# Two memory steps to a round from the ninth round on, memory scores kept to two PSUM banks, gate rows turned four to six steps earlier

## The chip, the cores and the metric

The kernel runs on one core of a Trainium2 chip. The metric is the device time of one launch in microseconds (us). The engines are called by their names and by the short names of the profile: TensorE (PE, its weight loads PEld), VectorE (DVE), ScalarE (ACT), GpSimd (POOL) and SyncE (SP), which issues most of the transfers.

## The reference, cut to what matters

The reference is a stack of three layers on 512 tokens of width 1024. The change touches the mixer of the last one only:

```
h = modulate(rms_norm(x, norm_mix_g), sh1, sc1)
q_a, k_a, v_a, qk_m, v_m, o_m, gates = split(h @ w_in)
y_attn = axial_gqa_attention(q_a, k_a, v_a, ...)      # 8 heads of 64, full softmax over 512 keys
y_mem = bidirectional_mlstm(qk_m, v_m, o_m, gates, ...)  # 4 heads of 128, forward and backward
mix = concatenate([y_attn, y_mem]) @ w_out
x = x + g1 * mix

# mLSTM of one head and direction, in its parallel form, as the kernel computes it:
F = cumsum(log_sigmoid(f)); M = cummax(i - F)
score[s, t] = (k[s] . q[t]) * 128**-0.5 * exp(i[s] - F[s] - M[t])   # where s is not past t
y[t] = (score[:, t] @ v) / max(|sum_s score[s, t]|, exp(-(F[t] + M[t])))
```

## The kernel before, in words

All engines run one program each, written in one order by hand; they meet only through semaphores, and each engine takes its own instructions in order. Tokens lie in T = 4 row blocks of 128.

**The projection w_in.** It is computed as a run of matrix products, in this order: k2 (8 blocks), conv 0 and 1 (4 blocks), og (8 blocks), conv 2 and 3 (4 blocks), v2 (8 blocks). A block is 12 matmuls of 512 columns in k2, og and v2 (lines 596 to 598; k2 is narrower) and 24 in conv (lines 622 to 624). After each block every engine takes one step of a generator `small_jobs` of 32 steps, numbered 0 to 31, so og holds steps 12 to 19, conv 2 and 3 steps 20 to 23, and v2 steps 24 to 31. In these steps sit: turning the gate rows on TensorE (`gates`, line 1104, steps 17 and 18) after VectorE wrote the log of the forget gates ("lf", line 2552, step 12); copying them on ScalarE (steps 18 and 19); the two scans of each direction on VectorE (`gates`, lines 2515 to 2525, steps 24 and 26), the SiLU of the convolutions on ScalarE (line 1681, steps 15 and 25), turning the gate columns on TensorE (`gate_columns`, lines 1114 and 1115, steps 28 and 30), their copy and exp on ScalarE (lines 1669 and 1670, steps 29 and 31), and the first two steps of attention (steps 28 and 30).

**Attention (`heads`).** A step u of `attend("B")` on TensorE issues two score products of 512 columns (line 848), the turning of two exponentiated score rows of step u-2 (line 857, `turn_p`) and, when u is odd, the product with v for two row blocks (line 873). VectorE takes the row maximum bound of the two scores (line 2148) and copies one of the turned rows (line 2163), ScalarE does exp (line 1436) and the other copy (line 1380). There are 16 pairs of scores, and TensorE has 21 steps in all. VectorE's write of a score row waits for the turning of the row four before it, in the same step of TensorE.

**Memory (`memory`).** Eight passes m (head and direction, even m forward, odd m backward) of four steps t. Step (m, t) on TensorE issues the score product of row block t (`score`, line 1168; 512, 384, 256, 128 columns for t = 0 to 3 when m is even, the other way round when m is odd), at t = 0 and 2 the outcome of the pass before for two row blocks (`outcome`, line 1182), and at t = 2 the broadcast of the next running maximum (`start`, line 1160). On VectorE, step (m, t) is `weigh` (lines 2607 and 2610: score times decay, read from the bank), at t = 1 and 3 also `divide` of the pass before (lines 2619, 2621, 2629 or 2632: it reads the outcome's bank), and at t = 3, ahead of `weigh`, `own` of the next pass (line 2592). ScalarE makes the decays (lines 1763 and 1770), GpSimd masks the diagonal (line 2863).

**The round.** `side_by_side` takes one step of `heads` and one of `memory` in turn on each engine until both have ended. Rounds are numbered here from 0, so round n has attention step u = n + 2 and, on all engines, memory step k = n - 1, where k = 4m + t. Attention ends on TensorE with round 18, and 18 memory steps follow alone.

**PSUM banks.** A bank is taken as the least recently used of a set: attention's scores and turned rows from banks 0 to 3, its outcome from 4, the running maximum from 5, and memory's scores and outcomes from 6 and 7. Once `heads` has ended on TensorE (`busy` is empty), memory's scores and outcomes are taken from banks 0 to 4, 6 and 7 (`B_LATE`). Before writing into a bank, TensorE waits for the engine that read its last user: `weigh` for a score, the second half of `divide` for an outcome.

**Weight chunks.** A weight chunk of 128x2048 is split by ScalarE (line 1278) and VectorE (line 1906) into two halves. In `memory` at step k = 12 both engines prepare one chunk ahead for the product that follows (`cur.reach(high, 2)`, `cur.reach(low, 2)`).

Of the kernel before, what the change touches and what calls it, by code (L numbers as in the profile page):

```python
# [188 lines left out]

def side_by_side(heads, mem, over):  # L190

    live = [heads, mem]
    while live:
        for job in (heads, mem):
            if job in live and next(job, over) is over:
                live.remove(job)


def weight_plan(a_w_in, a_w_o, b_w_in, b_w_o, mlp_w_up, mlp_w_down, w_ada_2, w_in_2, w_out_2, w_gate_2, w_up_2, w_down_2):
# [98 lines left out]
def program(nc, x, positions, a_w_in, a_w_o, b_w_in, b_w_a2, b_b_a, b_g_norm, b_w_o, ln_mix_g, ln_mix_b,  # L298
# [4 lines left out]
    with ctx:  # L303
# [169 lines left out]

        LAG = 2

        B_UNITS, B_OUT, B_MAX, B_MEM, B_LATE, ANY = range(4), (4,), (5,), (6, 7), (0, 1, 2, 3, 4, 6, 7), range(8)

        DIVIDED = {"A": 7, "B": 4}

# [70 lines left out]
        def tensor_program(pe):  # L550
# [572 lines left out]
            def small_jobs():  # L1123
                for step in range(32):
                    if step == 10:
                        turn("qT2", tm, 4, s_step.at("rope q"))
                    if step in (17, 18):
                        gates(step - 17)
                    if step == 20:
                        turn("kT2", kd2, 2, s_step.at("rope k"))  # L1130
                    if step in (28, 30):
                        gate_columns((step - 28) // 2)
                    if step in (28, 30):
                        next(heads)
                    yield
# [8 lines left out]
            gemm_tok("v2", 512, "x4", 1, among=range(4, 8))  # L1144
            drain(jobs)

            busy = ["heads"]

            def until_done(heads):
                yield from heads  # L1150
                busy.clear()

            def memory():
                def start(m):
                    hh, d = MEM[m]
                    b = banks.take(("M", m), False, B_MAX)
                    sel = ident[32 * d:32 * d + 4, 32 * d + hh:32 * d + hh + 1].broadcast_to([4, P])
                    w.wait_ge(*banks.free(("M", m), s_act.sem))
                    w.wait_ge(*s_step.at(("Mr", d)))
                    pe.matmul(bank[b][:, :], sel, Mr[d], start=True, stop=True).then_inc(*s_mm.up(("M", m)))  # L1160

                def score(m, t):
                    hh = MEM[m][0]
                    c0, c1_ = keys(m, t)
                    b = banks.take(("S", m, t), False, B_MEM if busy else B_LATE)
                    w.wait_ge(*banks.free(("S", m, t), s_act.sem))
                    w.wait_ge(*s_act.at(("conv", 7)))
                    pe.matmul(bank[b][:, 0:c1_ - c0], mqk[:, 4 + hh, t * P:(t + 1) * P], mqk[:, hh, c0:c1_],
                              start=True, stop=True).then_inc(*s_mm.up(("S", m, t)))

                def outcome(m, tt):
                    hh, d = MEM[m]
                    b = banks.take(("hm", m, tt), False, B_MEM if busy else B_LATE)
                    w.wait_ge(*banks.free(("hm", m, tt), s_act.sem))
                    w.wait_ge(*s_step.at(("ST", m, T - 1)))
                    w.wait_ge(*s_act.at(("v2", T - 1)))
                    w.wait_ge(*s_step.at("vx1"))
                    for t in (2 * tt, 2 * tt + 1):
                        src = list(range(0, t + 1) if d == 0 else range(t, T))
                        o = (t % 2) * 256  # L1180
                        for q in src:
                            step = pe.matmul(bank[b][:, o:o + 130], STm[m % 2][:, q, t * P:(t + 1) * P], vx[:, q, hh, :],
                                             start=q == src[0], stop=q == src[-1])
                    step.then_inc(*s_mm.up(("hm", m, tt)))

# [11 lines left out]
            side_by_side(until_done(heads), memory(), jobs)  # L1197
# [54 lines left out]
        def scalar_program(act):  # L1252
# [430 lines left out]
            def small_jobs():  # L1683
                for step in range(32):
# [15 lines left out]
                    if step in (18, 19):  # L1700
                        gates(step - 18)
# [4 lines left out]
                    if step in (29, 31):  # L1706
                        gate_columns((step - 29) // 2)
                    if step in (28, 30):
                        next(heads)
                    yield  # L1710
# [158 lines left out]
        def vector_program(dve):  # L1869
# [667 lines left out]
            def small_jobs():  # L2537
                for step in range(32):
# [18 lines left out]
                    if step in (24, 26):  # L2557
                        gates((step - 24) // 2)
                    if step in (28, 30):
                        next(heads)  # L2560
                    yield
# [437 lines left out]
```

## Time and profile before

| | us |
|---|---|
| median of 3 runs | 1908.58 |
| lowest and highest | 1908.34 and 1909.94 |
| the profiled execution, its own time | 1908.34 |
| its span in the profile | 1906.6 |
| PE busy | 1848.9 (97%) |
| DVE busy | 1151.6 (60%) |
| ACT busy | 734.6 (39%) |
| POOL busy | 108.8 (6%) |

The profiled execution took 1908.34 us, 1.74 us more than its span, and 0.24 us less than the median. The chain that ended last runs for 77% of the span over TensorE, for 15% over VectorE and for 4% over ScalarE. TensorE's granted clock was 0.994 over the span. The attention and memory rounds lie between 1363.6 and 1476.2 us of the span; the products of w_in before them.

### The profile page before, as it was taken

Reading aid. Unit: us, or ns where it says so; the run is one execution under the profiler, and the core shown is the slowest. Engines: PE = TensorE matmul, PEld = TensorE weight load, DVE = VectorE, ACT = ScalarE, POOL = GpSimd, SP = SyncE. Lnnn points to the kernel's source line nnn. Section 1 sums busy time; section 2 is a strip of 40 time slices with the busy share of each in tenths; the row PEclk is TensorE's granted clock in tenths of the full one; section 3 lists DMA queues with packets and bytes.
Section 4 is the critical chain, followed back from the end, with each engine's and each line's share of the span. In section 5 each row is a group of like instructions: output and inputs, shape, how many; then the busy total and the mean of one; then the engine's idle time right before and its main releaser. Section 6 shows DMA issues by size and latency. Waiting matters only on the chain.

```text
span 1906.6 us, 22855 instructions
## 1 busy us (share of the span) xinstructions
PE 1848.9 (97%) x9156; PEld 1495.3 (78%) x9156; DVE 1151.6 (60%) x2038; ACT 734.6 (39%) x1155; POOL 108.8 (6%) x109
## 2 busy tenths in 40 slices
PE   9999999999999999999999999899988999999997
PEld 7775888878888888878888888688655798888885
DVE  4987676555557686567554544976666554333438
ACT  4458352233233434544322222365554352222221
POOL 0341000000000152000000000000001000000000
PEclk9999999999999999999999999999999999999999
DMA  6221425433432121233434343122100313223221
GB/s 207 67 72 35 161 89 173 158 133 133 149 138 91 62 72 45 66 133 107 137 112 131 111 132 111 46 90 88 67 17 28 100 34 121 89 95 104 89 89 45
DMA packets 119018, 187.24 MB, mean 98 GB/s; under 512 B 7664, under 2 KB 72400, under 8 KB 115840
## 3 DMA queue, kind: packets, MB, share of 16 engines
q1 hardware_dynamic: 117520, 180.96, 28.9%
q0 software_dynamic: 1392, 4.82, 0.8%
q8 instruction: 72, 1.18, 0.3%
q14 instruction: 34, 0.28, 0.0%
HBM read 183.62 MB, written 2.15 MB: 97 GB/s over the span
## 4 chain that ended last, share of the span: by engine, by line
PE 77%; DVE 15%; ACT 4%; issue 3%; DMA 1%; POOL 0%; DVEq 0%; SPq 0%; ACTq 0%; POOLq 0%
PE bank L622 10%; PE bank L624 10%; PE bank L623 10%; PE bank L815 7%; PE bank L813 7%; PE bank L814 7%; PE bank L596 2%; PE bank L598 2%; PE bank L597 2%; DVE wl L1906 2%; PE bank L873 2%; DVE gb L2259 2%; PE bank L848 2%; PE bank L857 2%; DVE m L2257 1%
## 5 line engine op out<-in xcount | busy, mean ns | idle before, releaser
L1906 DVE TENSOR_TENSOR wl<-raw,wh 128x2048 fp32r<-128x2048 f32 (+1 forms) x137 | 308.2, 2254 | 190.7 <-ACT wh L1278 190.1
L1278 ACT ACTIVATE wh<-raw 128x2048 fp32r<-128x2048 f32 (+1 forms) x142 | 265.1, 1882 | 227.9 <-PE bank L815 90.4
L622 PE MATMUL bank<-xh,wh 128*128 128x512 f32 (+1 forms) x872 | 343.0, 393 | 4.0 <-DVE wl L1906 4.0
L623 PE MATMUL bank<-xh,wl 128*128 128x512 f32 (+1 forms) x872 | 342.2, 392 | 0.0
L624 PE MATMUL bank<-xl,wh 128*128 128x512 f32 (+1 forms) x872 | 342.2, 392 | 0.0
L815 PE MATMUL bank<-wh,ul 128*128 128x512 f32 x592 | 230.5, 389 | 0.0
L814 PE MATMUL bank<-wl,uh 128*128 128x512 f32 x592 | 230.4, 389 | 0.0
L813 PE MATMUL bank<-wh,uh 128*128 128x512 f32 x592 | 230.4, 389 | 0.0
L622 PEld LDWEIGHTS bank<-xh,wh 128*128 128x128 f32 (+1 forms) x872 | 163.5, 187 | 43.2 <-DVE wl L1906 5.1
L624 PEld LDWEIGHTS bank<-xl,wh 128*128 128x128 f32 (+1 forms) x872 | 163.5, 187 | 37.4
L623 PEld LDWEIGHTS bank<-xh,wl 128*128 128x128 f32 (+1 forms) x872 | 163.5, 187 | 36.7
L596 PE MATMUL bank<-wh,xh 128*128 128x512 f32 (+1 forms) x352 | 138.3, 393 | 1.7 <-DVE wl L1906 1.7
L2073 DVE TENSOR_TENSOR h<-h,bank 128x512 f32<-128x512 f32 x112 | 75.4, 683 | 105.1 <-PE bank L815 102.1
L1400 ACT ACTIVATE A<-bank 128x512 f32<-128x512 f32 x64 | 38.2, 596 | 259.0 <-PE bank L624 255.4
L598 PE MATMUL bank<-wh,xl 128*128 128x512 f32 (+1 forms) x352 | 134.1, 381 | 0.0
L597 PE MATMUL bank<-wl,xh 128*128 128x512 f32 (+1 forms) x352 | 133.9, 380 | 0.0
L814 PEld LDWEIGHTS bank<-wl,uh 128*128 128x128 f32 x592 | 111.1, 188 | 23.3
L813 PEld LDWEIGHTS bank<-wh,uh 128*128 128x128 f32 x592 | 111.2, 188 | 23.2
L815 PEld LDWEIGHTS bank<-wh,ul 128*128 128x128 f32 x592 | 111.1, 188 | 23.2
L2082 DVE TENSOR_TENSOR A<-A 128x512 f32<-128x512 f32 x64 | 44.1, 689 | 93.7 <-ACT A L1400 93.4
L1380 ACT ACTIVATE A<-bank 128x512 f32<-128x512 f32 (+4 forms) x106 | 51.4, 489 | 88.8 <-PE bank L598 32.3
L596 PEld LDWEIGHTS bank<-wh,xh 128*128 128x128 f32 x352 | 66.2, 188 | 16.6 <-issue 2.6
(352 smaller groups left out, 2962.6 us busy)
## 6 DMA issues: line engine op xcount, KB each, us to landing
raw<-in_mlp_w_up SPq DMA_DIRECT2D x32, 1024.0 KB, 5.6
raw<-in_mlp_w_down SPq DMA_DIRECT2D x32, 1024.0 KB, 5.1
raw<-in_w_ada SPq DMA_DIRECT2D x24, 1024.0 KB, 5.0
raw<-in_b_w_in SPq DMA_DIRECT2D x12, 1024.0 KB, 5.3
raw<-in_w_gate SPq DMA_DIRECT2D x11, 1024.0 KB, 5.3
raw<-in_w_up SPq DMA_DIRECT2D x11, 1024.0 KB, 5.5
raw<-in_w_in SPq DMA_DIRECT2D x10, 1024.0 KB, 5.1
raw<-in_w_down SPq DMA_DIRECT2D x10, 1024.0 KB, 5.0
```

The costliest lines, as they stand in the source:

```text
L596: pe.matmul(o, X, H[:, k, :], start=kk == 0, stop=False)
L597: pe.matmul(o, X, L[:, k, :], start=False, stop=False)
L598: step = pe.matmul(o, Y, H[:, k, :], start=False, stop=kk == 7)
L622: pe.matmul(o, H[:, k, c], xh[:, k, :], start=k == 0, stop=False)
L623: pe.matmul(o, L[:, k, c], xh[:, k, :], start=False, stop=False)
L624: step = pe.matmul(o, H[:, k, c], xl[:, k, :], start=False, stop=k == 7)
L813: pe.matmul(o, X, H[:, f, :], start=f == 0, stop=False)
L814: pe.matmul(o, X, L[:, f, :], start=False, stop=False)
L815: step = pe.matmul(o, Y, H[:, f, :], start=False, stop=f == nf - 1)
L1278: act.activation(slots[slot_of[i]][0][:, 0:n], raw[:, i % NRAW, 0:n], ACT.Copy).then_inc(*s_high.up(i))
L1906: dve.tensor_tensor(L[:, 0:n], raw[:, i % NRAW, 0:n], H[:, 0:n].bitcast(F), ALU.subtract).then_inc(*s_low.up(i))
L2073: dve.tensor_tensor(hv, hv, ps, ALU.add).then_inc(*s_row.up(name))
```

## The change

Three edits, on all engines that have a part in them:

1. `side_by_side` takes one memory step to an attention step in the first eight rounds and two from round 8 on.
2. The set `B_LATE` is gone: memory's scores and outcomes are taken from banks 6 and 7 to the end, also when attention has ended.
3. In `small_jobs`, TensorE turns the gate rows in steps 13 and 14 (17 and 18 before) and the gate columns in steps 22 and 26 (28 and 30); ScalarE copies the rows in steps 14 and 15 (18 and 19) and does the columns in steps 23 and 27 (29 and 31); VectorE scans in steps 20 and 24 (24 and 26).

```
--- before.py
+++ after.py
@@ -189,11 +189,12 @@
 
 def side_by_side(heads, mem, over):
 
-    live = [heads, mem]
+    live, n = [heads, mem], 0
     while live:
-        for job in (heads, mem):
+        for job in (heads, mem) if n < 8 else (heads, mem, mem):
             if job in live and next(job, over) is over:
                 live.remove(job)
+        n += 1
 
 
 def weight_plan(a_w_in, a_w_o, b_w_in, b_w_o, mlp_w_up, mlp_w_down, w_ada_2, w_in_2, w_out_2, w_gate_2, w_up_2, w_down_2):
@@ -473,7 +474,7 @@
 
         LAG = 2
 
-        B_UNITS, B_OUT, B_MAX, B_MEM, B_LATE, ANY = range(4), (4,), (5,), (6, 7), (0, 1, 2, 3, 4, 6, 7), range(8)
+        B_UNITS, B_OUT, B_MAX, B_MEM, ANY = range(4), (4,), (5,), (6, 7), range(8)
 
         DIVIDED = {"A": 7, "B": 4}
 
@@ -1124,12 +1125,12 @@
                 for step in range(32):
                     if step == 10:
                         turn("qT2", tm, 4, s_step.at("rope q"))
-                    if step in (17, 18):
-                        gates(step - 17)
+                    if step in (13, 14):
+                        gates(step - 13)
                     if step == 20:
                         turn("kT2", kd2, 2, s_step.at("rope k"))
-                    if step in (28, 30):
-                        gate_columns((step - 28) // 2)
+                    if step in (22, 26):
+                        gate_columns((step - 22) // 4)
                     if step in (28, 30):
                         next(heads)
                     yield
@@ -1144,12 +1145,6 @@
             gemm_tok("v2", 512, "x4", 1, among=range(4, 8))
             drain(jobs)
 
-            busy = ["heads"]
-
-            def until_done(heads):
-                yield from heads
-                busy.clear()
-
             def memory():
                 def start(m):
                     hh, d = MEM[m]
@@ -1162,7 +1157,7 @@
                 def score(m, t):
                     hh = MEM[m][0]
                     c0, c1_ = keys(m, t)
-                    b = banks.take(("S", m, t), False, B_MEM if busy else B_LATE)
+                    b = banks.take(("S", m, t), False, B_MEM)
                     w.wait_ge(*banks.free(("S", m, t), s_act.sem))
                     w.wait_ge(*s_act.at(("conv", 7)))
                     pe.matmul(bank[b][:, 0:c1_ - c0], mqk[:, 4 + hh, t * P:(t + 1) * P], mqk[:, hh, c0:c1_],
@@ -1170,7 +1165,7 @@
 
                 def outcome(m, tt):
                     hh, d = MEM[m]
-                    b = banks.take(("hm", m, tt), False, B_MEM if busy else B_LATE)
+                    b = banks.take(("hm", m, tt), False, B_MEM)
                     w.wait_ge(*banks.free(("hm", m, tt), s_act.sem))
                     w.wait_ge(*s_step.at(("ST", m, T - 1)))
                     w.wait_ge(*s_act.at(("v2", T - 1)))
@@ -1194,7 +1189,7 @@
                         if m + 1 < len(MEM) and t == 2:
                             start(m + 1)
 
-            side_by_side(until_done(heads), memory(), jobs)
+            side_by_side(heads, memory(), jobs)
             UH, UL = (v[:, :, :, :].rearrange("p a f s -> p (a f) s") for v in (uh, ul))
 
             def u_ready(k):
@@ -1697,14 +1692,14 @@
                         act.activation(g2_[:, :, :], g2_[:, :, :], ACT.Ln).then_inc(*s_act.up("g log"))
                     if step == 11:
                         turned_to("qT2", 4, qT2)
-                    if step in (18, 19):
-                        gates(step - 18)
+                    if step in (14, 15):
+                        gates(step - 14)
                     if step in (15, 25):
                         silu_owed()
                     if step == 21:
                         turned_to("kT2", 2, kT2)
-                    if step in (29, 31):
-                        gate_columns((step - 29) // 2)
+                    if step in (23, 27):
+                        gate_columns((step - 23) // 4)
                     if step in (28, 30):
                         next(heads)
                     yield
@@ -2554,8 +2549,8 @@
                         next(rope_k, None)
                     if step == 19:
                         dve.memset(vx[:, :, :, 128:130], 1.0).then_inc(*s_step.up("vx1"))
-                    if step in (24, 26):
-                        gates((step - 24) // 2)
+                    if step in (20, 24):
+                        gates((step - 20) // 4)
                     if step in (28, 30):
                         next(heads)
                     yield
```

## Rows read from the trace of the kernel before

**Rows 1.** Windows of the rounds: busy of each engine, then PEclk, DMA share, GB/s.

```profile
1402.40:1438.30 35.90, 28.87 (x180) 17.53 (x179) 22.68 (x61) 22.34 (x56) 3.82 (x4) 0.99 0.03 9
1438.30:1476.20 37.90, 35.88 (x190) 23.86 (x191) 23.52 (x84) 12.94 (x44) 3.81 (x5) 0.92 0.12 36
```

**Rows 2.** TensorE's timeline in rounds 8 and 9: start, duration, line, operation, count.

```profile
1403.48 1.09 PE L857 MATMUL bank<-C,pl 128*128 128x128 f32 x8
1404.41 1.02 PE L1168 MATMUL bank<-A 128*128 128x512 f32 x2
...
1408.13 1.95 PE L873 MATMUL bank<-xf,A 128*64 128x256 f32 x16
1410.00 1.13 PE L1168 MATMUL bank<-A 128*128 128x512 f32 x2
```

**Rows 3.** VectorE's timeline in round 8.

```profile
1404.26 0.75 DVE L2148 TENSOR_SCALAR_CACHE_REDUCE pl<-bank,q_rms 128x512 f32<-128x512 f32 x1 [3.72 <-PE bank L857]
...
1405.60 0.69 DVE L2163 COPY xf<-bank 128x512 f32<-128x512 f32 x1
1406.21 0.68 DVE L2177 TENSOR_TENSOR ul<-pl,uh 128x512 fp32r<-128x512 f32 x1
1406.81 0.68 DVE L2592 SCALAR_TENSOR_TENSOR rz<-bank,acol 128x512 f32<-128x512 f32 x1
1407.41 0.55 DVE L2607 SCALAR_TENSOR_TENSOR xf<-bank,C 128x384 f32<-128x384 f32 x1
...
1408.07 0.21 DVE L2619 TENSOR_TENSOR den<-den,ecol 128x2 f32<-128x2 f32 x1
...
1409.04 0.74 DVE L2148 TENSOR_SCALAR_CACHE_REDUCE pl<-bank,q_rms 128x512 f32<-128x512 f32 x1
```

**Rows 4.** VectorE's timeline, a memory step in the tail.

```profile
1453.06 0.42 DVE L2607 SCALAR_TENSOR_TENSOR xf<-bank,rz 128x256 f32<-128x256 f32 x1 [1.45 <-PE bank L1168]
...
1453.60 0.15 DVE L2619 TENSOR_TENSOR den<-den,ecol 128x2 f32<-128x2 f32 x1
```

**Rows 5.** TensorE's timeline after its longest wait in the rounds.

```profile
1438.33 0.37 PE L883 MATMUL bank<-C,att 128*8 128x128 f32 x1 [4.08 <-DVE att L2155]
1438.63 3.68 PE L873 MATMUL bank<-xf,A 128*64 128x256 f32 x16
```

**Rows 6.** Windows of 2 us behind three waits of TensorE.

```profile
1224.00:1226.00 2.00, 2.00 (x6) 1.54 (x5) 1.76 (x10) 0.00 (x0) 0.00 (x0) 0.51 0.55 193
...
1440.00:1442.00 2.00, 2.00 (x12) 0.92 (x8) 0.83 (x3) 0.00 (x0) 0.00 (x0) 0.50 0.04 10
...
1518.00:1520.00 2.00, 2.00 (x14) 1.74 (x13) 1.08 (x2) 0.85 (x1) 0.00 (x0) 1.00 0.03 8
```

**Rows 7.** TensorE's waits between 1205 and 1250 us: total, times, longest.

```profile
PE bank L1093 <- DVE xl L1959: 6.4, 3, 3.0
```

**Rows 8.** TensorE's timeline: start of og, of v2's first two blocks, attention's third step.

```profile
1291.77 0.39 PE L596 MATMUL bank<-wh,xh 128*128 128x512 f32 x1
...
1338.01 0.39 PE L596 MATMUL bank<-wh,xh 128*128 128x512 f32 x1
...
1340.73 0.39 PE L596 MATMUL bank<-wh,xh 128*128 128x512 f32 x1
...
1364.60 1.13 PE L848 MATMUL bank<-A 64*128 64x512 f32 x4 [0.93 <-ACT ecol L1670]
```

**Rows 9.** VectorE's timeline in og and v2.

```profile
1299.47 0.22 DVE L2552 SCALAR_TENSOR_TENSOR g_<-gg,g_ 128x64 f32<-128x64 f32 x1
...
1345.05 0.48 DVE L2515 MEMSET A<- 4x512 f32 x1
...
1349.61 0.48 DVE L2515 MEMSET A<- 4x512 f32 x1 [0.16 <-issue]
```

**Rows 10.** ScalarE's timeline in v2.

```profile
1341.48 1.28 ACT L1681 ACT_TABLE_LOAD   x1
1342.78 2.20 ACT L1681 ACTIVATE A<-A 128x512 f32<-128x512 f32 x4
```

More of the change, by code:

```diff
@@ L190, in side_by_side @@
 def side_by_side(heads, mem, over):
-    live = [heads, mem]
+    live, n = [heads, mem], 0
     while live:
-        for job in (heads, mem):
+        for job in (heads, mem) if n < 8 else (heads, mem, mem):
             if job in live and next(job, over) is over:
                 live.remove(job)
+        n += 1
 def weight_plan(a_w_in, a_w_o, b_w_in, b_w_o, mlp_w_up, mlp_w_down, w_ada_2, w_in_2, w_out_2, w_gate_2, w_up_2, w_down_2):
@@ L474, in program @@
         LAG = 2
-        B_UNITS, B_OUT, B_MAX, B_MEM, B_LATE, ANY = range(4), (4,), (5,), (6, 7), (0, 1, 2, 3, 4, 6, 7), range(8)
+        B_UNITS, B_OUT, B_MAX, B_MEM, ANY = range(4), (4,), (5,), (6, 7), range(8)
         DIVIDED = {"A": 7, "B": 4}
@@ L1126, in small_jobs @@
                         turn("qT2", tm, 4, s_step.at("rope q"))
-                    if step in (17, 18):
-                        gates(step - 17)
+                    if step in (13, 14):
+                        gates(step - 13)
                     if step == 20:
                         turn("kT2", kd2, 2, s_step.at("rope k"))
-                    if step in (28, 30):
-                        gate_columns((step - 28) // 2)
+                    if step in (22, 26):
+                        gate_columns((step - 22) // 4)
                     if step in (28, 30):
@@ L1145, in tensor_program @@
             drain(jobs)
[L1147 to L1151, printed above, removed]
             def memory():
@@ L1164, in score @@
                     c0, c1_ = keys(m, t)
-                    b = banks.take(("S", m, t), False, B_MEM if busy else B_LATE)
+                    b = banks.take(("S", m, t), False, B_MEM)
                     w.wait_ge(*banks.free(("S", m, t), s_act.sem))
@@ L1172, in outcome @@
                     hh, d = MEM[m]
-                    b = banks.take(("hm", m, tt), False, B_MEM if busy else B_LATE)
+                    b = banks.take(("hm", m, tt), False, B_MEM)
                     w.wait_ge(*banks.free(("hm", m, tt), s_act.sem))
@@ L1195, in memory @@
                             start(m + 1)
-            side_by_side(until_done(heads), memory(), jobs)
+            side_by_side(heads, memory(), jobs)
             UH, UL = (v[:, :, :, :].rearrange("p a f s -> p (a f) s") for v in (uh, ul))
@@ L1699, in small_jobs @@
                         turned_to("qT2", 4, qT2)
-                    if step in (18, 19):
-                        gates(step - 18)
+                    if step in (14, 15):
+                        gates(step - 14)
                     if step in (15, 25):
@@ L1705, in small_jobs @@
                         turned_to("kT2", 2, kT2)
-                    if step in (29, 31):
-                        gate_columns((step - 29) // 2)
+                    if step in (23, 27):
+                        gate_columns((step - 23) // 4)
                     if step in (28, 30):
@@ L2556, in small_jobs @@
                         dve.memset(vx[:, :, :, 128:130], 1.0).then_inc(*s_step.up("vx1"))
-                    if step in (24, 26):
-                        gates((step - 24) // 2)
+                    if step in (20, 24):
+                        gates((step - 20) // 4)
                     if step in (28, 30):
```

## The prediction

> **What bounds the kernel now.** I read the page first: TensorE is busy for 97% of the span and carries 77% of the chain that ended last, so a microsecond is won or lost only where TensorE waits or where its clock is low. The windows of the rounds come next, since the change rearranges only these and the last steps ahead of them [rows 1]. Between 1402.40 and 1476.20 us TensorE is idle for 7.03 and 2.02 us, 9.05 in all; the mean clock of the second window is 0.92, which over 37.9 us is 3.0 us of full-speed work lost. So these 73.8 us have 12.1 us of slack, and that is nearly all that edits 1 and 2 can win. Rounds 0 to 7 keep their order, so they are left out.
>
> The timelines say what kind of rounds these are. In round 8 TensorE turns the score rows at 1403.48 and issues memory's score at 1404.41 [rows 2]. VectorE starts on the round 0.78 us after the turning, at 1404.26, and goes through both maxima, the copy, a split (line 2177), `own` and `weigh`, and only then `divide`, which ends at 1409.04 [rows 3]. TensorE does not mind, because a whole attention step lies between this score and memory's next one at 1410.00 [rows 2]. This cover is what edit 1 removes.
>
> **Edits 1 and 2, banks first.** Memory's scores and outcomes alternate over banks 6 and 7, so each one takes the bank of the use before last. In the order S(m,0), O(m-1,0), S(m,1), S(m,2), O(m-1,1), S(m,3), S(m+1,0), O(m,0) that gives two waits to look at: S(m,2) needs the bank of O(m-1,0), which VectorE frees with `divide` in step (m,1); and S(m+1,0) needs the bank of O(m-1,1), freed by `divide` in step (m,3). Before, an attention step of TensorE stood between. From round 8 on a round holds steps k = 7 and 8, 9 and 10, and so on: the pairs are (m,3) with (m+1,0) in even rounds and (m,1) with (m,2) in odd ones. Both pairs put the `divide` and the score that waits for it into one round. Behind the waiting score stand the outcome, the next running maximum and the whole next attention step, since TensorE takes its instructions in order.
>
> *Even rounds.* In round 8 the order up to S(1,3) is the same as before, so its price can be read off directly. S(1,3) starts at 1404.41 and takes 1.02 us, to 1405.43; `divide` ends at 1409.04 [rows 2, 3]. S(2,0) can't start earlier: 3.6 us of wait. Round 12 has the same parts, 3.6 again. Round 10 has no split on VectorE (0.60, from 1406.21 to 1406.81) and a shorter `weigh` (about 0.2 for 0.66), but also a score of 128 columns instead of 512 on TensorE (about 0.6 less): 3.2. From round 14 on there are no new attention scores, so the two maxima (1.34, from 1404.26 to 1405.60) and then the rest of attention fall away on VectorE; rounds 14, 16 and 18 come to about 2.2, 1.8 and 1.4. Together 15.8 us.
>
> *Odd rounds.* The product with v (1.95 [rows 2]) covers VectorE's attention part. What can't be covered is the chain S(m,1), `weigh`, `divide`, S(m,2): `weigh` of 256 and 128 columns took 0.54 from 1453.06 to 1453.60 [rows 4], `divide` 0.97 from 1408.07 to 1409.04 [rows 3], and I add 0.15 for the two hand-overs, an estimate. 1.65 us each, in rounds 9, 11, 13, 15 and 17: 8.2 us.
>
> *The chunk.* The preparation at k = 12 now falls in round 10, and VectorE's part, which has to wait for ScalarE's, stands ahead of round 11's maxima. In the trace before, the same work cost TensorE its longest wait, 4.08 us [rows 5]. I put round 11's wait at 4.1 in place of 1.65: 2.5 more. *The tail.* Three rounds of memory alone on two banks add about 2.3 (one wait as in an odd round, and `weigh` of the last score, 0.7). The sum of TensorE's waits from round 8 on is 15.8 + 8.2 + 2.5 + 2.3 = 28.8 us, against 9.05 before: **+19.7 us**. The work itself does not change.
>
> There is a rule that speaks against edit 2. The Trainium skill, page "Perfetto Trace Analysis", section "Matmuls", says that independent matmul groups should rotate through different PSUM banks so that reading one overlaps the next group's products. By that rule the seven banks should stay for the whole double stretch, and with them the waits above would mostly be gone; the wait in the tail before is small, 2.02 us in 37.9, which agrees.
>
> **Clock.** After the wait of 4.08 us the granted clock was 0.50 (1.2 GHz), and 16 matmuls with v took 3.68 us for 1.95 [rows 2, 5, 6]. After the longest of three waits that make 6.4 us together it was 0.51; after a shorter wait, ahead of 1518, it stayed at 1.00 [rows 6, 7]. So waits of this length are followed by a slow spell often, not always: three of four in this trace that I looked at. The 3.0 us of before [rows 1] go away with their wait. In the new order six waits have 2.5 us or more (four here, two below). I take 4.5 spells of 1.7 us, and 0.6 of that on the path, since these rounds wait anyway: +4.6, net **+1.6 us**. The bounds are 0 and 6 x 3.0 = 18 for the spells.
>
> **Edit 3.** *Gate rows.* og starts at 1291.77 and a block takes 2.72 us (1338.01 to 1340.73) [rows 8]. Step 13 comes after two blocks, at 1297.2. The turning needs "lf", which VectorE began to write at 1299.47, for 0.22 us [rows 9]. In steps 17 and 18 that was long past; in step 13 TensorE waits **2.5 us**. ScalarE's copies wait in turn, and with them its SiLU and its next chunk, by some 5 us as I count the steps. That chunk is for conv 2, which starts only when og's eight blocks are through, 21.8 us after 1291.77 and later than 1313; VectorE, 60% busy in the page, makes up the rest before conv 3. I cost it at nothing; without that cover it would be what reaches past og's end, 0 to 2 us.
>
> *Gate columns.* The scans of one direction take 4.4 us (1345.05 to 1349.45, with the next start at 1349.61) [rows 9]. The first direction moves to step 20, where VectorE has idle time: nothing. The second stays where VectorE started scanning before, at 1345.05, because it stands behind conv 7 and a chunk's split. But TensorE's turning moves from step 30 to step 26, three blocks into v2: 1338.01 + 8.16 = 1346.2 [rows 8]. The scans end at 1349.45, 0.16 before the next start. With 0.3 more on VectorE, because a table load of ScalarE (1.28 [rows 10]) now stands ahead of the chunk: **3.6 us** of wait, bounds 3.2 and 5. *Gain.* Attention's third step waited 0.93 us for the columns' exp on ScalarE, whose bank it takes [rows 8]; that goes: **-0.9**. Two more table loads, 2.6 us, lie in idle time of ScalarE but for what is counted. Net +5.2 us, if neither wait overlaps the other; both shift what follows by the same amount, so they add.
>
> ScalarE's load in v2 is followed by the SiLU after 1.30 us [rows 10]. The Trainium skill, page "ScalarE: Activation LUTs", section "What ACT_TABLE_LOAD costs", adds a drain of 1.38 us to each switch. The two rows leave no room for one behind the load; if it stood ahead of the load that is on the chain, the second wait would be 5.0 and the sum 1.4 us more.
>
> **The sum**, made against the profiled execution's own 1908.34 us (0.24 below the median): 1908.3 + 19.7 + 1.6 + 5.2 = 1934.8, say **1935 us**, 1.4% slower.
>
> **The rivals.**
> *It works as intended.* The second memory step fills TensorE's waits instead of making new ones. Its place is the second score of a round: it would need `divide` to be over when TensorE gets there, so at least 3.6 us of other TensorE work between the two scores in even rounds. The profile has none there, and only a freed bank could bring it. It would win the 9.05, the 3.0 and the 0.9, with edit 3's waits at nothing: 1895.4 us. Chance 0.05.
> *Half of the waits.* Edit 3 hurts nobody (gain 0.9) and only the waits of the even rounds and of the tail appear: 18.1 - 9.05 = +9.1, clock -3.0 + 2.0: 1908.3 + 9.1 - 1.0 - 0.9 = 1915.5 us. For it speaks that VectorE, 60% busy, might run nearer to TensorE than I count. Chance 0.12.
> *The clock decides.* Each of the six waits is followed by a spell as long as the one of before, all on the path: 18 for 4.6, 1948 us. For it: 3 of 4. Against it: the spells elsewhere were shorter. Chance 0.13.
> *No change* that a measurement can tell (within 0.2%, 3.8 us, which is about its limit here): the waits just replace the old ones. The even rounds' 3.6 us is read directly, so this needs many errors of mine at once. Chance 0.05.
>
> **How the numbers follow.** My forecast has 0.65, its own range is 1925 to 1943 (the second gate wait, the odd rounds' estimate and the spells). The range that holds 8 in 10 takes in half of each slow rival: 1915 to 1946. Slower by over 0.2%: 0.65 + 0.12 + 0.13 = 0.90; within 0.2%: 0.05; faster: 0.05.
>
> **What would show it.** In the profile after: TensorE idle ahead of line 1168 in rounds 8 to 18, released by VectorE's `divide` (lines 2629 and 2632), 15 to 25 us in total with a longest of 3.5 to 4; idle ahead of line 1104 for 2.5 released by line 2552; ahead of line 1114 for about 3.6 released by the last op of the scans (line 2525 in the numbering of before); attention's last score later than before, the end of the rounds near 1500 instead of 1476; more than one slow spell. The prediction is wrong if the waits ahead of line 1168 are absent or short, or if VectorE reaches `divide` before its attention part, which its order does not allow.

## The result and the profile after

The changed kernel took 1952.09 us (median of 4 runs, 1951.55 to 1955.71), beside 1909.26 us for the kernel before in the same comparison: a ratio of 1.0227, 95% interval 1.0209 to 1.0245. It is 43 us slower. I had said 1935 us, 1915 to 1946: the direction and the waits were right, the time is 17 us above the forecast and 6 above the range.

The profiled execution took 1955.38 us with a span of 1953.6, 47.0 us more than before's. It is 3.3 us above the median: three of the other four took 1951.6 to 1952.2 us at a granted clock of 0.985 over the span, and this one had 0.982. So the profile shows somewhat more low clock than the median run has. Lines of TensorE up to the rounds count one higher than before, those of the memory steps and of the other engines five lower (1168 is now 1163, 1182 is 1177, 2629 and 2632 are 2624 and 2627). The view of TensorE's waits: total, times, longest.

```profile
PE bank L1163 <- DVE A L2624: 12.7, 6, 3.8
PE bank L1163 <- DVE A L2627: 12.0, 6, 3.3
...
PE bank L1115 <- DVE A L2520: 3.7, 1, 3.7
PE bank L884 <- DVE pl L2143: 3.2, 3, 2.2
...
PE bank L1105 <- DVE g_ L2547: 2.5, 1, 2.5
...
PE bank L1177 <- DVE A L2624: 1.8, 1, 1.8
```

These are the forecast waits, in their places: 24.7 us in twelve waits of memory's scores for `divide`, the chunk's in round 11, edit 3's two, and the tail's last. Round 8 in the timelines, TensorE first, shows how one comes about.

```profile
1413.49 1.02 PE L1163 MATMUL bank<-A 128*128 128x512 f32 x2
1418.27 2.08 PE L1163 MATMUL bank<-A 128*128 128x512 f32 x2 [3.75 <-DVE A L2624]
```

VectorE in the same round:

```profile
1413.35 0.75 DVE L2143 TENSOR_SCALAR_CACHE_REDUCE pl<-bank,q_rms 128x512 f32<-128x512 f32 x1 [3.72 <-PE bank L858]
...
1415.30 0.68 DVE L2172 TENSOR_TENSOR ul<-pl,uh 128x512 fp32r<-128x512 f32 x1
1415.89 0.69 DVE L2587 SCALAR_TENSOR_TENSOR rz<-bank,acol 128x512 f32<-128x512 f32 x1
1416.49 0.55 DVE L2602 SCALAR_TENSOR_TENSOR xf<-bank,C 128x384 f32<-128x384 f32 x1
...
1417.61 0.61 DVE L2624 TENSOR_SCALAR A<-bank,den 128x128 f32<-128x128 f32 x2
```

VectorE does the same list as in [rows 3], at the same pace. The first score runs 1413.49 to 1414.51, the second has to wait to 1418.27, 3.75 us (3.6 forecast). But that second score then takes 2.08 us where the first took 1.02: TensorE runs at half its clock (0.50 from 1417.5 to 1422.5). The windows of the whole affected part (busy of each engine, PEclk, DMA share, GB/s; the third is rounds 8 to 20):

```profile
1290.00:1341.00 51.00, 48.53 (x224) 39.47 (x223) 33.98 (x58) 25.08 (x32) 0.00 (x0) 0.97 0.21 69
1341.00:1411.50 70.50, 61.94 (x308) 39.63 (x307) 38.14 (x83) 37.79 (x79) 2.54 (x3) 0.98 0.15 52
1411.50:1521.60 110.10, 81.49 (x372) 50.95 (x371) 47.13 (x145) 35.82 (x100) 7.51 (x9) 0.80 0.05 15
1521.60:1953.00 431.40, 415.73 (x1954) 348.15 (x1953) 203.53 (x307) 124.20 (x142) 0.58 (x1) 0.99 0.26 85
```

The first, second and last of these in the kernel before, the end of the second being the start of its round 8:

```profile
1290.00:1341.00 51.00, 51.00 (x239) 42.02 (x238) 32.57 (x57) 27.93 (x35) 0.00 (x0) 1.00 0.27 88
1341.00:1402.40 61.40, 55.63 (x294) 34.95 (x292) 39.52 (x85) 33.22 (x76) 2.54 (x3) 1.00 0.13 43
...
1476.20:1906.00 429.80, 414.15 (x1955) 346.98 (x1953) 203.40 (x308) 124.21 (x142) 0.58 (x1) 0.99 0.26 85
```

Before, the rounds from 8 on took 73.8 us: 64.75 busy and 9.05 idle [rows 1]. Now they take 110.1: 81.49 busy with nearly the same number of instructions (372 for 370), and 28.61 idle. So of the 47.0 us, 19.6 are added idle time there, 16.7 are the same work at a lower clock, 9.1 are gathered before round 8 starts (1411.5 for 1402.4), and 1.6 come later.

Where the clock goes is seen in windows of rounds 10 and 11:

```profile
1435.50:1439.50 4.00, 1.50 (x7) 1.50 (x8) 2.67 (x11) 2.32 (x7) 1.87 (x2) 0.72 0.00 0
1439.50:1443.50 4.00, 4.00 (x14) 2.27 (x14) 0.30 (x1) 2.78 (x6) 0.00 (x0) 0.50 0.00 0
1443.50:1447.50 4.00, 1.79 (x14) 0.96 (x14) 4.00 (x7) 1.31 (x3) 0.00 (x0) 0.92 0.00 0
1447.50:1463.50 16.00, 14.51 (x43) 7.86 (x38) 3.91 (x14) 3.31 (x10) 0.00 (x0) 0.50 0.05 17
```

and in TensorE's timeline:

```profile
1438.00 0.79 PE L1163 MATMUL bank<-A 128*128 128x128 f32 x2 [3.33 <-DVE A L2627]
...
1446.22 0.27 PE L884 MATMUL bank<-C,att 128*8 128x128 f32 x1 [2.21 <-DVE pl L2143]
...
1451.71 1.65 PE L1163 MATMUL bank<-A 128*128 128x384 f32 x2 [1.49 <-DVE A L2624]
1453.15 3.24 PE L1177 MATMUL bank<-A,xf 128*128 128x130 f32 x14
```

A wait of 3.33 us that ends at 1438.00 is followed by a spell at 0.50 (1.2 GHz). The clock comes back around 1444, the chunk's wait of 2.21 begins at the same time, another of 1.49 falls into the next spell, and the engine stays at 1.2 GHz for at least 16 us. I had counted spells that lose 1.7 us each, with 0.6 of that on the path.

Edit 3's two waits in TensorE's timeline:

```profile
1299.90 0.60 PE L1105 MATMUL bank<-C,gg 128*4 128x128 f32 x4 [2.47 <-DVE g_ L2547]
...
1355.12 0.22 PE L1115 MATMUL bank<-C,A 4*128 4x4 f32 x1 [3.72 <-DVE A L2520]
```

2.47 and 3.72 us for 2.5 and 3.6 forecast; the 0.93 of [rows 8] is gone. That makes 5.3 of the 9.1 us ahead of round 8. Most of the other 3.8 shows as 0.97 and 0.98 in the first two windows above, where before has 1.00: an estimate from these is 0.03 x 51.0 + 0.02 x 70.5 = 2.9 us.

### The profile page after: what moved, and what is told of

It reads as the page before. It is cut to its first block, busy times and chain, and to the rows that moved or that the text cites. A ratio compares the mean times of both kernels' runs of the same rounds, so it can differ in the third digit from the quotient of the medians.

```text
span 1953.6 us, 22854 instructions
## 1 busy us (share of the span) xinstructions
PE 1871.2 (96%) x9156; PEld 1508.1 (77%) x9156; DVE 1153.3 (59%) x2038; ACT 736.9 (38%) x1156; POOL 108.6 (6%) x109
## 4 chain that ended last, share of the span: by engine, by line
PE 76%; DVE 16%; ACT 4%; issue 3%; DMA 1%; POOL 0%; DVEq 0%; SPq 0%; ACTq 0%; POOLq 0%
PE bank L623 10%; PE bank L625 10%; PE bank L624 10%; PE bank L815 7%; PE bank L816 7%; PE bank L814 6%; DVE wl L1901 2%; PE bank L597 2%; PE bank L599 2%; PE bank L598 2%; PE bank L849 2%; PE bank L858 2%; PE bank L874 2%; DVE gb L2254 2%; DVE m L2252 1%
```

## The experiments

"Idle" and "busy" are TensorE's in the stretch from the start of round 8 to the first product behind the rounds, from the windows of each run's own profile.

| run | time (us) | ratio to before, 95% | idle + busy in the stretch |
|---|---|---|---|
| before | 1909.3 to 1911.9 | | 9.1 + 64.8 |
| after | 1952.09 | 1.0227 (1.0209 to 1.0245) | 28.6 + 81.5 |
| edit 3 alone | 1920.31 | 1.0052 (1.0037 to 1.0067) | 9.0 + 65.2 |
| edit 1 alone | 1940.23 | 1.0158 (1.0141 to 1.0175) | 27.3 + 78.9 |
| edit 2 alone | 1922.44 | 1.0067 (1.0052 to 1.0082) | 19.8 + 66.2 |
| edits 1 and 2 | 1942.29 | 1.0169 (1.0154 to 1.0184) | 29.7 + 72.5 |
| after, divide first | 1934.79 | 1.0123 (1.0099 to 1.0147) | 14.7 + 76.3 |
| after, other pairs | 1928.64 | 1.0096 (1.0079 to 1.0112) | 13.9 + 68.9 |
| before, chunk later | 1909.88 | 0.9992 (0.9983 to 1.0002) | 8.4 + 64.9 |
| before, divide first | 1910.76 | 1.0002 (0.9992 to 1.0011) | 10.4 + 66.0 |
| after, all waits filled | 1944.24 | 1.0176 (1.0160 to 1.0192) | filled: see below |
| after, score waits filled | 1943.61 | 1.0181 (1.0167 to 1.0194) | filled: see below |
| after, round 11 filled | 1955.50 | 1.0230 (1.0216 to 1.0243) | filled: see below |
| edit 3 alone, waits filled | 1917.50 | 1.0037 (1.0024 to 1.0049) | filled: see below |
| before, three waits filled | 1912.59 | 1.0008 (1.0000 to 1.0016) | filled: see below |
| before, chunk's wait filled | 1909.81 | 1.0000 (0.9991 to 1.0009) | filled: see below |
| before, doubled from round 9, divide first | 1911.02 | 1.0000 (0.9990 to 1.0010) | 9.3 + 64.0 |

**Which edit costs what.** Four runs: edit 3 alone (only the lines of the gates), edit 1 alone, edit 2 alone, edits 1 and 2. Edit 1 alone:

```diff
-    live = [heads, mem]
+    live, n = [heads, mem], 0
     while live:
-        for job in (heads, mem):
+        for job in (heads, mem) if n < 8 else (heads, mem, mem):
             if job in live and next(job, over) is over:
                 live.remove(job)
+        n += 1
```

Edit 2 alone is `B_MEM` for `B_MEM if busy else B_LATE` at both places.

> The kernel before with edit 3 alone. The theory (waits of TensorE, and slow clock behind them, add up): two waits, 2.5 us ahead of the gate rows and 3.7 ahead of the gate columns, less 0.9 gained, and 3 to 4 us of slow clock behind them: 1915 to 1919 us. The rival (the time sits in the rounds alone, edit 3 is hidden): 1908 us within 2.

> Edit 1 alone, the late banks kept. The theory (the wait arises in rounds where attention still runs and memory has banks 6 and 7): 26 of the 28.6 us of waits stay, 9 of before go, clock loss of 12 to 17 us: 1936 to 1944 us. The rival (the loss of the late banks is what costs): 1900 to 1912 us.

> Edit 2 alone, one memory step to a round. The theory: the 18 steps that run alone now wait for the divide in every second step, about 9 waits of 1.6 us in place of 2.0 us in all: +12 us, clock loss 0 to 5 more: 1919 to 1926 us. The rival (only the doubled rounds suffer): 1908 us within 3.

> Edits 1 and 2 without edit 3. The theory: the 43 us of the change less the 9 us that edit 3 put ahead of the rounds: 1941 to 1945 us. If it is below 1935, the three edits feed each other (the gate waits bring the rounds into a slow clock).

Edit 3 costs 10 us by itself, 1.3 more than the upper end expected; the other three came out inside theirs. Edit 1 is the dear one, +30. Edit 2 costs 13 alone but little on top of edit 1, since most of its waits are there with edit 1 too; edits 1 and 2 and edit 3 add up to the whole (33 + 10 for 43). The stretches of edit 1, of edit 2 and of both, one row from the windows of each run:

```profile
1405.90:1512.10 106.20, 78.93 (x371) 50.07 (x371) 46.93 (x144) 35.84 (x100) 7.51 (x9) 0.82 0.05 16
```

```profile
1404.70:1490.70 86.00, 66.21 (x372) 41.43 (x371) 46.75 (x145) 35.51 (x100) 7.62 (x9) 0.96 0.06 19
```

```profile
1404.50:1506.70 102.20, 72.51 (x372) 46.13 (x371) 47.02 (x144) 35.84 (x100) 7.51 (x9) 0.90 0.05 16
```

Edit 2's added waits, all of 1.5 to 1.8 us, lie in rounds of memory alone and add 10.7 us of idle time but only 1.5 us to busy: the clock stayed at 0.96. With both edits the waits are those of after (3.75, 1.63, 3.33, 2.21, 1.49 in rounds 8 to 11), yet busy is 72.5 there and 81.5 in after's profile. In both the clock comes back to 1.00 about when the wait of 2.21 begins; in after it falls again behind this wait, with both edits alone it does not:

```profile
1438.23 0.27 PE L884 MATMUL bank<-C,att 128*8 128x128 f32 x1 [2.21 <-DVE pl L2149]
```

```profile
1436.50:1453.50 17.00, 10.02 (x53) 5.67 (x54) 9.89 (x28) 7.10 (x17) 0.63 (x1) 1.00 0.06 16
```

So the price of the clock isn't fixed by the list of waits. Part of the difference is the spread from one execution to the next: after's profiled execution is 3.3 us above its median, this one (1940.47) is 1.8 below its own, and by the medians the two kernels are 9.8 us apart, about what edit 3 costs alone.

**Divide first.** The waits end with `divide`, so it is put at the head of VectorE's memory step, in after and, as a control, in before.

```diff
+                        if m and t % 2:
+                            divide(m - 1, t // 2)
                         if m + 1 < len(MEM) and t == 3:
                             own(m + 1)
                         if m < len(MEM):
                             weigh(m, t)
-                        if m and t % 2:
-                            divide(m - 1, t // 2)
```

> The changed kernel, with VectorE's divide ahead of own and weigh in a memory step. The theory (the second score waits for the divide of its own round): the waits of the odd rounds nearly vanish (TensorE's product with v covers the divide), those of the even rounds keep the outcome's wait for weigh, about 17 us of waits for 28.6, and the clock loss falls by more than in proportion, by about 8 us: 1929 to 1937 us. Rival A (clock loss is tied to the rounds, not to the waits): 1940 us. Rival B (it is not the divide that is waited for): 1952 us.

> The kernel before, with the divide ahead of own and weigh. The theory: with one step to a round the divide is covered by the attention step, so nothing changes: 1908 us within 3. If it is faster by over 4 us, the order on VectorE costs something in itself and the reading of the run with divide first has to allow for it.

Both times came out. VectorE's timeline in round 8 of this version of after:

```profile
1417.20 0.68 DVE L2172 TENSOR_TENSOR ul<-pl,uh 128x512 fp32r<-128x512 f32 x1
...
1418.19 0.61 DVE L2624 TENSOR_SCALAR A<-bank,den 128x128 f32<-128x128 f32 x2
1418.71 0.68 DVE L2587 SCALAR_TENSOR_TENSOR rz<-bank,acol 128x512 f32<-128x512 f32 x1
```

and TensorE's:

```profile
1418.85 1.12 PE L1163 MATMUL bank<-A 128*128 128x512 f32 x2 [2.43 <-DVE A L2624]
```

`own` and `weigh` now follow, and the wait is 2.43 us in place of 3.75. Idle time in the stretch is halved, 14.7 for 28.6, 2 us less than expected. The clock's part is not: busy is still 76.3, 11.6 above before, so it fell by 5.2 us where I expected 8. Each of the four waits of 2.4 to 2.7 us left in the rounds has a spell of low clock behind it, and so has one of 1.48 us (0.51 from 1471.5 to 1478.5).

**Other pairs.** `n < 9` for `n < 8` makes the pairs (m,0) with (m,1) and (m,2) with (m,3); no pair then holds a `divide` and the score that waits for it.

> The changed kernel with the doubling from round 9 instead of 8, so that the pairs of a round are (m,0) with (m,1) and (m,2) with (m,3), and the divide that a score waits for lies in the round before. The theory: the waits of the rounds fall from 28.6 us to 4 to 10, the slow clock nearly goes, edit 3 keeps its 9 us: 1910 to 1920 us. The rival (two memory steps in a round are too much for VectorE or for two banks in any pairing): 1945 us or more.

A miss: 1928.6 lies 9 us above the upper end of the theory, though far below the rival. Edit 3's 9 us were in the expectation. The rest is in the rounds: idle is 13.9 us where 4 to 10 were expected, and busy 68.9, 4.1 above before, where the slow clock was nearly to go. The longest wait left is the chunk's, whose work still stands ahead of one `divide`:

```profile
1439.15 1.65 PE L1163 MATMUL bank<-A 128*128 128x384 f32 x2 [4.13 <-DVE A L2624]
```

Behind it come six more for `divide`, 0.76 to 1.76 us each, in the last rounds. Against after, the pairing alone takes 14.7 us off TensorE's idle time and 12.6 off its busy time.

**Chunk later.** Before, with both `cur.reach(..., 2)` at `m == 3` moved to `m == 6`.

> The kernel before, with the weight chunk of step k = 12 prepared at k = 24, when memory runs alone. The theory: the 4.1 us wait and the slow clock behind it (3.0 us) go, and VectorE's slack in the tail takes all but 0 to 2 us of it: 1901 to 1904 us. The rival (the wait only moves): 1908 us.

A miss: no change. The wait of 4.08 us is gone, and VectorE's same work is now late for another one. TensorE's waits:

```profile
PE bank L1182 <- DVE den L2619: 3.1, 1, 3.1
```

This one has its spell of low clock too: busy is 64.9, as before.

**Filling the waits.** Does the low clock come from these waits at all? Throwaway turnings of the identity keep TensorE at work in front of a waiting score, in a bank of attention's that is free at that time; they change nothing of when VectorE ends.

```diff
+                def fill(n):
+                    if n:
+                        f = next(c for c in banks.order if c in B_UNITS)
+                        w.wait_ge(*banks.read.get(banks.user[f], (s_act.sem, 0)))
+                    for _ in range(n):
+                        pe.transpose(bank[f][:, 0:P], ident, ident)
...
                     b = banks.take(("S", m, t), False, B_MEM)
+                    fill({8: 22, 10: 9, 12: 20, 14: 8, 16: 18, 18: 9, 20: 13, 22: 8, 24: 10, 26: 9, 28: 8, 30: 8}.get(4 * m + t, 0))
                     w.wait_ge(*banks.free(("S", m, t), s_act.sem))
```

> The changed kernel, with throwaway 128x128 turnings of the identity on TensorE in front of the waits for a bank in the doubled rounds: 22, 9, 20, 8, 18, 9, 13, 8, 10, 9, 8 and 8 of them ahead of the second scores of rounds 8 to 19, and 14 ahead of round 11's turning of the inverses. They stand in a free bank of attention's scores, last some 0.12 us each (8 took 1.09), so about three quarters of each wait, and change no wait of anything on VectorE. Theory, that the step of my prediction that failed is the clock term (81.5 us of work for 64.8 in rounds 8 to 20 of the changed kernel): the order and the ends of the waits stay, the granted clock of that stretch goes from 0.80 to 0.97 or more, and the time falls by 12 to 17 us, to 1935 to 1940 us. Rival, that the missing 17 us are something else that slows TensorE's work there (contention, reading of banks): the stretch keeps its length or grows by what of the filling doesn't fit, 1950 to 1960 us.

> As the run with all waits filled, but with only round 11's two waits filled (14 turnings ahead of the inverses, 8 ahead of the score of k = 14). In the changed kernel the clock was low from 1447 to 1463 us, behind those two waits of 2.2 and 1.5 us. Theory, that one slow spell is prolonged by the next wait that falls into it or right behind it: this alone gives back 4 to 8 us, 1944 to 1948 us. Rival, that how long a slow spell lasts is not set by the waits near it (without edit 3 the same waits lost 7.8 us in place of 16.7): the loss moves to other rounds, 1950 to 1954 us.

TensorE's timeline of the run with all waits filled:

```profile
1415.31 2.57 PE L1165 MATMUL bank<-C 128*128 128x128 f32 x22
...
1419.23 1.12 PE L1174 MATMUL bank<-A 128*128 128x512 f32 x2 [1.35 <-DVE A L2635]
...
1443.68 3.25 PE L885 MATMUL bank<-C 128*128 128x128 f32 x14 [4.03 <-DVE pl L2154]
```

The first two rows are as meant: 2.57 us filled, 1.35 left, and the score takes 1.12 us where it took 2.08. The third shows a mistake of mine: at round 11's inverses TensorE waits for the bank, and my filling stands behind that wait, not in it, at half clock, and costs 3.25 us. The run with only round 11 filled (1955.50 us, ratio 1.0230, 1.0216 to 1.0243) has the same mistake, so its time tells nothing of its question: whether filling this one wait would shorten the long spell was not tested. Its trace shows how much the clock varies. A line of TensorE's timeline, then two windows:

```profile
1437.85 0.49 PE L1174 MATMUL bank<-A 128*128 128x128 f32 x2 [3.33 <-DVE A L2638]
```

```profile
1450.00:1463.00 13.00, 9.13 (x54) 5.45 (x50) 6.30 (x20) 3.12 (x8) 0.64 (x1) 1.00 0.07 20
...
1504.50:1518.20 13.70, 10.51 (x31) 7.06 (x32) 5.07 (x16) 4.30 (x16) 1.87 (x2) 0.50 0.00 0
```

Up to round 10 this program is the same as after, and its waits are too. Yet the score behind the wait of 3.33 us ran at full clock here (0.49 us) and at half clock in after (0.79). The long spell behind round 11 is absent, and another of 13.7 us stands near the end, where nothing was filled. With the misplaced 14 left out and all the scores' fillings kept:

> The changed kernel with its waits for a bank ahead of the second scores filled with throwaway turnings as before, but without the 14 ahead of round 11's inverses. In the run with all waits filled these 14 stood behind the wait that they were to fill (a wait for the bank, 4.03 us), at a clock of 0.50, and cost 3.2 us of their own. Theory (the clock term): the clock in the doubled rounds stays at 0.95 or more and the time is 3 us below that run's 1944.2: 1939 to 1942 us. Rival (a low clock is not tied to TensorE's idle time, the gain of that run had another cause): 1944 or more.

1943.61 us, 8.8 us (1.0227 less 1.0181, of 1909.7) below after. It lies between the theory's upper end (1942) and the rival (1944 or more), and 0.6 us below the run with the misplaced filling, by the ratio no lower; by the time alone it doesn't decide between them. Both filled runs are 2 to 4 us above what I expected. The trace decides. The stretch in its windows:

```profile
1411.10:1508.40 97.30, 81.50 (x513) 56.64 (x513) 47.02 (x144) 35.75 (x100) 7.53 (x9) 0.96 0.05 17
```

97.3 us for 110.1, and the clock at 0.96 for 0.80. 142 fillings take 17.5 us of the busy time (the window of their line alone is below), so the kernel's own work is 64.0, about what it was before (64.75); idle is 15.8, and filled and idle together are 33.3, 4.7 more than after's idle 28.6. Part of the low clock's price in after was thus hidden in waits, since VectorE's end doesn't come later because TensorE is slow: in the profiled executions 17.5 us of work come back and 12.8 of time in this stretch, 11.8 over the whole run, and by the medians 8.8. The fillings' own window:

```profile
1411.10:1508.40 97.30, 17.52 (x142) 16.20 (x142) 0.96 0.05 17
```

**The same for edit 3.** Edit 3 alone with 18 and 26 turnings ahead of its two waits, each in the bank that it is about to write.

> Edit 3 alone, with its two new waits filled: 18 throwaway turnings ahead of the wait of 2.5 us for the log of the gates and 26 ahead of the wait of 3.7 us for the scans. Edit 3 alone took 1920.3 us where its waits less its gain come to 5.3 us; round 8 started 8.6 us later than before. Theory, that the missing 3.3 us are the clock behind the two waits (0.97 from 1290 to 1341 us, 0.98 from there to round 8): 1916 to 1918 us. Rival, that the rest of edit 3's price is elsewhere (a chunk made later, more loads of ScalarE's tables): 1919 to 1921 us.

1917.50 us, ratio 1.0037 (1.0024 to 1.0049), for 1920.31 and 1.0052: 2.8 us less, but the two intervals overlap, so the times alone don't show a gain. The windows do, first those of edit 3 alone:

```profile
1290.00:1341.00 51.00, 48.53 (x224) 39.46 (x223) 34.40 (x59) 25.07 (x32) 0.00 (x0) 0.97 0.21 66
1341.00:1411.10 70.10, 61.55 (x309) 39.33 (x307) 37.72 (x83) 37.79 (x79) 2.54 (x3) 0.98 0.15 52
```

and with its waits filled:

```profile
1290.00:1341.00 51.00, 50.59 (x250) 41.67 (x249) 35.49 (x60) 25.16 (x33) 0.00 (x0) 1.00 0.24 79
1341.00:1411.00 70.00, 63.90 (x338) 40.87 (x337) 38.20 (x86) 38.50 (x82) 2.54 (x3) 1.00 0.12 41
```

With the waits filled the clock is 1.00 in both windows, and round 8 starts at 1407.61 in place of 1411.06: 3.4 us, the part of edit 3's price that its waits don't explain.

**The same for before.** Two tries to win its 3.0 us of clock back.

> The kernel before, with throwaway turnings on TensorE inside three of its own waits: 30 ahead of the inverses at 1438.33 us (a wait of 4.08), 20 and 16 ahead of q2's first and third block (waits of 2.98 and 2.53), each in the bank that the waiting product itself will write. Nothing else changes. Theory of the clock: the spells of low clock at 1439 to 1445, 1221 to 1226 and 1240 to 1243 us go, some 3.0 + 1.5 + 1.6 us of full-speed work by the windows, 1903 to 1905 us against 1909. Rival, that the clock falls without regard to TensorE's idle time: no change, 1908 to 1911 us, or up to 1 us more where the filling outlasts its wait.

> The kernel before with 30 throwaway turnings (3.5 us) in the wait of 4.08 us itself, ahead of the last inverses. The run that was to do this put them at the inverses before, where no wait is: it cost 3.5 us there and left the wait and its slow spell (clock 0.66 from 1440 to 1450) as they were. Theory: the spell of low clock behind the wait goes, 3.0 us of full-speed work, 1905.5 to 1907.5 us against 1909 to 1911 of before. Rival: the clock falls in any case, 1909 to 1911 us.

Neither gained: 1912.59 us (1.0008, 1.0000 to 1.0016) and 1909.81 (1.0000, 0.9991 to 1.0009). The first had one filling at the wrong inverses, where hardly any wait is (0.50 us), and lost 3.5 us there; the wait of 4.08 stayed. Its other two, in the waits of q2, gave back 0.6 us in the profile where 3.1 were expected: from the last product ahead of them to the next block behind, 1215.06 to 1286.21 us became 1217.44 to 1288.01. In the timeline of the second

```profile
1436.06 5.16 PE L884 MATMUL bank<-C 128*128 128x128 f32 x30 [1.97 <-ACT xf L1383]
```

the 30 turnings start 2 us into the wait, because they need its bank, run mostly at a low clock (5.16 us, where the same 30 took 3.49 in the first try), and end at 1441.2, 2.9 us after the wait would have ended [rows 5]. The clock is back when the real work starts (1.00 from 1442 to 1450), and the filling has eaten what that gives. A filling of half the size was not tried.

**A candidate.** Before with doubling from round 9 on, late banks kept, divide first.

> A candidate from the runs so far: the kernel before with its gate steps and late banks, doubling of memory from round 9 on in place of round 8, and divide at the head of VectorE's memory step. By the runs so far, 1928.6 for the other pairs with all edits: minus some 10 for the gates, minus some 4 for the tail's waits on two banks: 1911 to 1917 us. If the waits of the tail and the chunk's 4.1 go as well, since memory's steps then lie beside attention's: 1904 to 1908. Rival that doubling itself costs, whichever pairs: 1920 or more.

1911.02 us beside 1911.47, ratio 1.0000 (0.9990 to 1.0010). In the stretch it has 9.3 us idle and 64.0 busy, for 9.1 and 64.8. Doubling the memory steps is thus no cost in itself; it wins nothing either. No version beat the kernel before.

## Why the prediction was wrong, step by step

**Right.** Edits 1 and 2: 28.8 us of waits from round 8 on forecast, 28.61 measured, +19.6 for +19.7; and nearly all are for `divide`, as the divide-first and other-pairs runs show. The even rounds 8, 10 and 14 had 3.75, 3.33 and 2.27 us for 3.6, 3.2 and 2.2, the odd ones 1.49 to 1.63 for 1.65. Round 12 had 2.67 for 3.6 in after's profile: its first score ran at half clock and took 0.9 us longer, and so the wait was that much shorter; with edits 1 and 2 alone it was 3.75. Round 11 had 2.21 and 1.49, together 3.7 for 4.1. The tail had 1.50 and 1.76, together 3.3 for 2.3: the last wait was for `divide` and not, as I had it, for `weigh` at 0.7. That the sum came out within 0.2 us is thus in part luck, since round 12's shortfall hides the tail's excess: with edits 1 and 2 alone the idle time was 29.7, and with the scores' waits filled, at a clock of 0.96, idle and filled time together were 33.3. Edit 3: 2.47 + 3.72 - 0.93 = 5.3 us of waits for 5.2. No further wait followed from ScalarE's chunk, and the second wait was 3.72 us. The Trainium skill, page "ScalarE: Activation LUTs", section "What ACT_TABLE_LOAD costs", adds a drain of 1.38 us, which by my estimate would have made it 5.0; this trace does not show one.

**The step that failed** is the clock term. I put it as "4.5 spells of 1.7 us, and 0.6 of that on the path ... +4.6, net **+1.6 us**", for six waits, two of them edit 3's. Measured in the profiled execution: +16.7 us in the rounds and +3.8 ahead of them, 20.5 net for 1.6; with the 3.0 that before had, 23.5 for 4.6. With 1.6 us in the rest of the run that is the whole difference between the sum's 26.5 us and the span's 47.0: 15.1 + 3.8 + 1.6 = 20.5. This execution is 3.3 us above the median, which is 17 above the forecast. Filling the scores' waits shows that this slow work comes from the waits: the clock went from 0.80 to 0.96 and the kernel's own work from 81.5 to 64.0 us.

Two things were wrong in it. The length of a spell: I took the 1.7 us from a 16-matmul block in [rows 5], while the windows of 1402.4 to 1476.2 gave 3.0 us of work lost behind one wait [rows 1]. Edit 3's two spells did cost 3.4 us, 1.7 each; the six in the rounds cost 16.7 + 3.0 us, 3.3 each. The number: I counted spells one by one, each behind a wait of 2.5 us or more of its own. The doubled rounds bring a wait every 4 to 15 us, and some land where the clock has only just come back, or not yet; there were six spells in the rounds and two behind edit 3's waits, one of them over 16 us long, and two of the six stand behind waits of 1.5 to 1.8 us. A clock of 0.80 over 110.1 us is about 44 us at 0.50 (0.20 x 110.1 x 2), where before, with 0.95 over 73.8, had about 7. The share on the path, 0.6, was not far off: filling the waits brought back 12.8 us of time for 17.5 us of work, 0.7. My rival "the clock decides" had 18 us for this, 1948 us, and was nearest; it got 0.13. The 18 was short of the 23.5 in the profile. Of the 18 only the upper bound was used, where the wait of before gave it as the plain reading: six waits by 3.0.

There was a rule for this too. The Trainium skill, page "TensorE: Matmul & The Clock Gate", section "A second HAM failure mode: psum-queue depth-cycling", says that small idle times between groups of matmuls that go round the banks can let the clock swing between its two levels, and that throughput falls by what is paid again and again. The trace agrees that the clock swings (0.80 over 110.1 us), with waits of 1.5 to 3.75 us; I had weighed only the rule on rotating banks.

**What stays open.** Which waits a low clock follows, and for how long. The same waits cost 7.8 us of busy time in the profile of edits 1 and 2 and 16.7 in after's, and the same wait of 3.33 us had a spell behind it in after and none in the run with round 11 filled. Rounds 10 and 11 suggest that a wait which falls into a spell prolongs it; that was not tested. Filled waits gave 8.8 us back by the medians and 11.8 in the profiled executions; after's lies 3.3 above its median, which is about the difference.

## What to carry to other kernels

Before two steps of a job are put back to back, look which release (here `divide`) the second waits for and where it stands on the other engine; a pair that holds both makes a wait in every round, and one position more or less (`n < 9`) took 23 us off the changed kernel here. Price each wait that TensorE gets at its length plus the whole spell of low clock that a like wait shows in the trace, give the sum a wide upper bound, since the same waits cost from 7.8 to 16.7 us here, and allow for spells behind shorter waits when they come close together. Work that is moved off one wait (the chunk) turns up at the next unless it has idle time to go to.

## What I had not expected of the hardware

Throwaway matmuls in a wait are worth time: 142 of them, 17.5 us of useless work, made the changed kernel 8.8 us faster. These ended inside their waits; where 30 outlasted theirs by 2.9 us, nothing was gained. Eight waits of 1.5 to 1.8 us, 13 us in all, went with only 1.5 us more busy time (edit 2 alone), while three waits of 1.5 to 3.3 us within 14 us (rounds 10 and 11) went with a clock of 0.50 for 16 us.
